# Prompt attention of a hybrid encoder step: TensorE makes the next scores before it turns the probabilities, not after

## What is computed

```python
# A: 6 query heads on 2 key heads, own chunk of 64 + 2 chunks before, learned sink
# B: 5 heads, own chunk + 8 chunks before
# C: 5 heads, causal over all rows, with a forget bias
s = einsum(q, k) * d ** -0.5 + bias        # masked to the band
p = exp(s - max); p = p / sum(p)           # A adds exp(sink - max) to the sum
o = einsum(p, v)                           # head width 64
```

## Time and profile before

| | us |
|---|---|
| median of 3 runs | 3451.3 (3449.65 to 3466.47) |
| the profiled execution | 3448.5, its span 3446.7 |
| prompt attention, layer 0 | from 373.8 to 600.7 |
| prompt attention, layer 1 | about 2084 to 2311 |

### The profile page before, as it was taken

How to read it: one execution, slowest core, us unless ns; L and a number is a source line. 1 busy time by engine, 2 the same in 40 slices (tenths; PEclk the granted TensorE clock), 3 DMA queues, 4 the chain that set the end, 5 groups by cost and what they waited for, 6 DMA issues and landing times. The chain is left out here.

```text
span 3446.7 us, 48399 instructions
## 1 busy us (share of the span) xinstructions
PE 2922.6 (85%) x19074; PEld 2796.9 (81%) x19074; DVE 1679.7 (49%) x3625; ACT 774.2 (22%) x1515; POOL 1254.7 (36%) x589
## 2 busy tenths in 40 slices
PE   2989799668389999999919997987686999999994
PEld 2989689358289999999919996974575999999993
DVE  8520687348843333333466107864566333333336
ACT  1210566231220000000121106653214100000002
POOL 2122695101334344434231217841123443344431
PEclk9999999579589999999959999997886999999997
DMA  4341111325211111111023301122340111111101
GB/s 187 120 136 45 26 47 36 122 80 191 104 49 37 49 49 49 37 49 49 13 92 129 128 26 33 49 70 82 132 142 25 50 48 37 49 49 48 37 25 63
DMA packets 115055, 240.09 MB, mean 70 GB/s; under 512 B 42308, under 2 KB 78696, under 8 KB 102676
## 3 DMA queue, kind: packets, MB, share of 16 engines
q1 hardware_dynamic: 114900, 238.02, 20.1%
HBM read 211.94 MB, written 33.80 MB: 71 GB/s over the span
## 5 line engine op out<-in xcount | busy, mean ns | idle before, releaser
L362 PE MATMUL psum<-u_lo,w_hi 128*128 128x352 f32 x2304 | 744.2, 323 | 0.0
L362 PE MATMUL psum<-u_hi,w_hi 128*128 128x352 f32 x2304 | 742.8, 322 | 1.0 <-ACT v_rows L864 0.6
L362 PE MATMUL psum<-u_hi,w_lo 128*128 128x352 f32 x2304 | 743.2, 323 | 0.0
L340 POOL CAST w_hi<-w_raw 128x2048 fp32r<-128x2048 f32 (+1 forms) x92 | 177.6, 1931 | 1264.1 <-DVEq L1742 357.2
L1745 DVE SCALAR_TENSOR_TENSOR acc_t<-psum,mods,acc_t 128x704 f32<-128x704 f32 (+2 forms) x768 | 401.2, 577 | 293.4 <-PE psum L362 293.4
L362 PE MATMUL psum<-h_hi,w_lo 128*128 128x352 f32 x1536 | 495.3, 322 | 0.0
L362 PE MATMUL psum<-h_lo,w_hi 128*128 128x352 f32 x1536 | 495.0, 322 | 0.0
L362 PE MATMUL psum<-h_hi,w_hi 128*128 128x352 f32 x1536 | 494.3, 322 | 0.0
L342 POOL TENSOR_TENSOR w_lo<-w_raw,w_hi 128x2048 fp32r<-128x2048 f32 (+1 forms) x92 | 457.4, 4971 | 7.4
L362 PEld LDWEIGHTS psum<-u_hi,w_hi 128*128 128x128 f32 x2304 | 433.0, 188 | 2.3 <-issue 2.0
L362 PEld LDWEIGHTS psum<-u_lo,w_hi 128*128 128x128 f32 x2304 | 433.2, 188 | 0.0
(11 more groups left out here) (211 smaller groups left out, 4848.6 us busy)
## 6 DMA issues: line engine op xcount, KB each, us to landing
w_raw<-in_w_all SPq DMA_DIRECT2D x86, 1024.0 KB, 4.8
w_ada_f<-in_w_ada_t SPq DMA_DIRECT2D x48, 512.0 KB, 3.3
w_ada_b<-in_w_ada_t SPq DMA_DIRECT2D x32, 512.0 KB, 3.3
scr_o<-o_head SPq DMA_DIRECT2D x32, 256.0 KB, 2.6
row_tiles<-scr_o SPq DMA_DIRECT2D x16, 512.0 KB, 7.1
w_raw<-in_w_v SPq DMA_DIRECT2D x6, 1032.0 KB, 12.8
w_ada_a<-in_w_ada_t SPq DMA_DIRECT2D x10, 512.0 KB, 17.9
bias<-scr_forget_new SPq DMA_DIRECT2D x10, 512.0 KB, 3.8
```

Of the source, the lines that this page charges most:

```text
L340: pool.tensor_copy(w_hi[s][:, 0:c], raw[s][:, 0:c]).then_inc(pool_step, 1)
L362: mm = pe.matmul(out[:, b, :], w[s][:, c:c + P], a[:, k, b * NB:(b + 1) * NB], start=(k == 0 and w is w_hi and a is a_hi), stop=(k == n - ...
```

## The change

Within a step TensorE issues the scores of item k+1 first, then the turn of item k-2, then the attend of item k-3. No instruction, wait, buffer or other engine's string is changed.

```diff
                     scores(0)
                     for k in range(LAST + 3):
+                        if k + 1 < LAST:
+                            scores(k + 1)
                         if 2 <= k < LAST + 2:
                             turn_probs(k - 2)
-                        if k + 1 < LAST:
-                            scores(k + 1)
                         if k >= 3:
                             attend(k - 3)
```

## The result

Over eight runs of each the changed kernel takes 3480.1 us (3473.2 to 3488.7) and the old one 3452.6 us. The ratio is 1.0071, with a 95% interval of 1.0055 to 1.0088: 0.7% slower, where 3469 us had been said. The profiled run, one of the longer ones, took 3485.6 us.

What follows compares the result with a forecast made beforehand. Bounds: VectorE in A heads, mostly a 2.19 us turn ring in B, TensorE in C. Losses of 3.1 (A), 3.3 (B), 2.3 (C) make 8.7 us a layer, 17.4 in two: 3451.3 becomes 3468.7, said as 3469; range 3455 to 3483.

Steps and rivals of the forecast that it cites:

- B spacings of 2.19 us four times and then 2.2 for 1.76: Turn-to-turn times in a B head: four stay 2.19 us, the one behind the 4-block item's turn becomes 2.20 from 1.76.
- a wait for `row_max` ahead of the next head's first turn: TensorE waits before the scores ahead of that turn, about 0.16 us in B heads and 0.44 us in C heads.
- Outside the attention nothing moves: Stages outside the prompt attention were to keep their times.
- A heads, 3.1 us a layer: Heads of 2-block items, one of 1 block: each loses 0.52 us, six heads 3.1 us a layer; head about 9.6 us.
- The ring: A heads, two steps: output, attend, turn, copy, split, output; scores inserted lengthen it from 2.16 to 2.38 us, past VectorE's 2.26.
- B heads, 0.60 a head: Heads with items of 5 down to 1 blocks: 0.44 us of moved score blocks plus 0.16 us wait for logits.
- The shift at T(4): B heads, turn of the 4-block item: four score blocks, 0.44 us, move into the stretch where TensorE is the bound.
- C heads, 0.65 a head: Heads with items of 8 down to 1 blocks: net 0.22 us of moved score blocks plus 0.44 us wait for logits.
- B to C: Step from the last B head to the first C head: costs 0.87 us, 0.44 + 0.43, with no part given back.
- The one that kept A heads at VectorE's pace: A heads stay at 1.13 us a step, only B and C heads lose, 11.2 us, 3462.5 in all; chance 0.16.
- The rival that the waits for `probs_lo` get filled: Scores run while a turn waits, so all 5.3 us a layer is filled: faster, 3441 us; chance 0.06.
- The rival of the clock: TensorE, idle more in A heads, is granted 1.2 GHz there: some 80 us more, 3530 us; chance 0.04.

Runs made afterwards that it cites:

- a_only: Old kernel with the scores moved ahead of the turn only while the turn belongs to an A head; ratio to the old kernel 1.0034.
- new_but_first: Old order in A heads; in B and C heads the changed order except in the step turning a head's first item; ratio to the old kernel 1.0025.
- second_first: Old kernel with scores first only in the step that turns the second item of a B or C head; ratio to the old kernel 0.9958.
- all_but_head0: Changed kernel, but with the old order while the turn belongs to the first head of a layer; ratio to the old kernel 1.0005.
- head0_only: Old kernel with the changed order only while the turn belongs to the first head of a layer; ratio to the old kernel 1.0002.
- balanced_after: Changed kernel with items of 5 or 6 blocks turned in groups of 3 and 2 (3 and 3), not 4 and 1 (4 and 2); ratio to old 1.0039.

## Why the prediction was right, and where its sizes were off

**The sign and the mechanism.** B spacings of 2.19 us four times and then 2.2 for 1.76, a wait for `row_max` ahead of the next head's first turn, and a longer wait at its second turn (0.78 us for 0.61 in B, 0.33 for 0.20 in C) all came. The A steps grew to 1.22 us in the mean, and VectorE waits for `probs_hi` there, but not visibly before each split: at full clock the view of waits lists it at about one split in eight, and the other gaps are too short for it. Two statements failed. "Outside the attention nothing moves": it moved by 9.4 us. And the clock did drop once, which the prediction had named as a sign of being wrong. The time, 3480, lies inside 3455 to 3483, near its upper end.

**A heads, 3.1 us a layer.** The ring was read as 2.38 us and is 2.42; the score link was 0.29 us instead of 0.22. The head was said to be about 9.6 and is 9.79. But the loss at full clock is 0.28 us a head, not 0.52, because the prediction counted from a head of VectorE's work alone, about 9.1 us. That is the shortest of the old ones, which run from 9.1 to 9.7. What makes most of the others longer is the denominators' sum at a head's end. Before, with the GpSimd record that it begins under, and after:

```profile
2137.43 1.03 POOL L1032 CAST queries<-qk_t 64x1024 fp32r<-64x1024 f32 x1 [0.17 <-POOL keys_lo L1025]
...
2137.76 0.72 DVE L1206 TENSOR_TENSOR denominator<-denominator,exp_sink 128x8 f32<-128x8 f32 x1
```

```profile
2143.55 0.16 DVE L1206 TENSOR_TENSOR denominator<-denominator,exp_sink 128x8 f32<-128x8 f32 x1
```

In the old kernel two of the four heads that the table averages end so, 0.57 us later each than with 0.15 us. The head of 9.56 us waits 0.35 us for GpSimd's masks ahead of its logits at 2115.03 us, and 0.1 in its sum. In layer 1 of the changed kernel none of these heads has a sum longer than 0.16 us. So the ring costs 0.68 us a head against 9.11, more than was said, and the 0.40 us that an old head lost to GpSimd in the mean hides more than half of it. With the dearer first head (+1 to 1.4) the layer pays 2.4 us: a_only. That this comes near the predicted 3.1 is in part luck: a ring mis-sized by 0.16 us a head, a saving and a start that the sum did not have.

**B heads, 0.60 a head.** Measured 0.78. The shift at T(4) is 0.47 us for the 0.44 said. The logits' release came when it was worked out, 4.22 us after T(3), and the wait was the 0.16 us. But T(1) to T(5) grew by 0.29, not 0.16. Most of the other 0.13 us is what the new neighbours cost: the attend follows T(1) after 0.13 us (492.58), where the scores followed it after 0.06, and its four matmuls take 0.48 us instead of 0.44 until the scores are due. The string of scores is no longer than it was. The old one, and the new one behind its wait:

```profile
450.62 0.48 PE L1068 MATMUL psum<-keys_hi,queries 128*128 128x512 f32 x1
...
450.93 0.40 PE L1068 MATMUL psum<-keys_lo,queries 128*128 128x512 f32 x1
```

```profile
493.56 0.39 PE L1068 MATMUL psum<-keys_lo,queries 128*128 128x512 f32 x1
```

From the first score matmul to the second it is 0.31 us in the one and 0.33 in the other (493.23 to 493.56), and to whatever follows the scores 0.72 and 0.73. The reason given for the 0.44 was incomplete: new_but_first shows that a string of VectorE and ScalarE behind T(3), and not only TensorE's work, keeps the time from being won back.

**C heads, 0.65 a head.** Measured 0.88. T(1) to T(8) took 1.71 us, 0.05 more than the 1.66 that the terms give. T(2) to T(1) took 1.83 for 1.68: the scores there, too, start only when the logits of the next head's first item have been read, which the prediction did not look at. The two spacings that were to give back 0.11 us each, T(7) to T(6) and T(6) to T(5), gave 0.06 and 0.08. T(8) to T(7) is 2.19 for 2.23. B to C was said to cost 0.87 and cost 1.17; the last C head gave back 0.5, not 0.3. B and C together are 7.3 us a layer, where the sum had 5.6; with A's 2.4 it is 9.7 us for its 8.7.

**The rivals.** The one that kept A heads at VectorE's pace falls, and with it the estimate from the figure of the Trainium skill for a single matmul ("TensorE: Matmul & The Clock Gate", section "Single matmul latency"), which the page gives for a bf16 matmul: the measured link from turn to copy is 0.48 us here, not 0.34. The rival that the waits for `probs_lo` get filled falls as a whole, but is right in one step, which second_first isolates. The rival of the clock has its price in the wrong place. Warm A heads of the new order keep 2.4 GHz in a_only and all_but_head0; the rise at the start of a layer may come 6 to 14 us later and may be lost once more. In the profiled run that is 16.4 + 11.3 less 19.4, 8.3 us. I had named the clock with 0.04 and left it out of the sum. So the time lies in the range for two reasons, and the sum had only one of them: by the rings and strings alone it would have been about 3472 us.

**What stays open.** In wall time the change costs 27.5 us between medians, 19 to 30 by the interval of the ratio; 19.4 are the rings and strings, read in two layers and reproduced part by part. Against the old kernel's medians on the other chips it would be 20 to 23. The rest goes with the clock, in the attention and outside. Outside it no instruction differs, and yet those stages took between 2987.6 and 3008.8 us in the 14 profiles. Nearly all of that is the sample attention, here from its first to its last record of logits. Layer 1, before and then after:

```profile
2325.87:2411.46 85.59, 63.57 (x379) 35.51 (x376) 38.30 (x158) 27.53 (x76) 12.78 (x4) 0.70 0.26 86
```

```profile
2349.53:2447.32 97.79, 77.25 (x374) 40.23 (x373) 38.43 (x160) 27.30 (x76) 12.78 (x4) 0.59 0.21 70
```

The same instructions took 84 to 99 us, at mean granted clocks of 0.70 down to 0.59. Both layers together took from 168.6 us (all_but_head0) to 189.6 (second_first); 173.9 before and 186.8 after, which is more than the 9.4 us above. Without them the time outside the attention is 2815 to 2821 us in all 14 profiles. all_but_head0 kept 17.6 us of the loss in its trace and lost nothing measurable in time, and that was no single good run: its ten runs have granted clocks of 0.915 to 0.918, the 26 runs of the old kernel beside it 0.907 to 0.917, 0.912 in the mean. So how the sample attention is clocked seems to go with the kernel, though its instructions are the same in all. What in the stage before it decides this no run shows, and so the changed order's share in it stays open.

## What to carry to other kernels

When several engines pass items in a ring, an instruction moved ahead of another's input lengthens each ring that passes between its new neighbours. List the rings, sum each one's links from start to start, and compare them with the busiest engine's own step before moving anything. A wait on the busiest engine is worth filling only in the step where it stands and only if the turn behind is not itself what the ring waits for. If a ring is the bound, cut its largest link: smaller first groups gave more than any order did. Look at the engines beside the path, too: here GpSimd's records took back more than half of what the longer ring cost in the A heads.

## What the hardware showed that was not expected

- A string of score matmuls is slow from its first to its second, also without a wait: 0.31 us behind a turn (450.62 to 450.93 us before the change), 0.28 behind an attend (488.32 to 488.60 after it), 0.33 behind an attend and a wait of 0.16 us (493.23 to 493.56), against 0.22 within the string. The wait so adds 0.05 us to its own length.
- VectorE's sum of two small SBUF tensors, 0.15 us by itself, took up to 2.33 us when it began under a GpSimd record, and ended 0.01 to 0.04 us behind that record. An order on TensorE that shifts VectorE by some tenths of a microsecond so gained or lost up to 2.2 us a head.
- With scores ahead of the turn at the start of a layer, the granted clock rose after 9 to 10 us in three starts (a_only in both layers, head0_only in layer 0), after 15 to 16 in three (head0_only, the changed kernel and balanced_after in layer 1) and after 23 in two (the last two in layer 0), where it also fell back from 2.4 to 1.2 GHz some 10 us later. With the old order there it rose after 8 to 10 us in 18 of 18.
- The sample attention, with unchanged instructions, took from 84 to 99 us a layer, at mean granted clocks of 0.70 and 0.59. That is nearly the whole spread of 21 us in the some 3000 us outside the prompt attention.
